# Norms between stages: column halves of the second tile, weights under the root, roots on ScalarE and VectorE

## The reference, cut to what matters

```python
def rms_norm(x, g):                       # and rmsnorm of the second block
    return x * rsqrt(mean(x * x, -1) + EPS) * g

for l in range(DEPTH):                    # first block
    x = x + rms_norm(hybrid_mixer(rms_norm(x, mix_pre), ...), mix_post)
    x = x + rms_norm(memory_cross_attention(rms_norm(x, mem_pre), ...), mem_post)
    x = x + rms_norm(squared_relu_mlp(rms_norm(x, mlp_pre), ...), mlp_post)
h = concat(meta, x)                       # second block, 16 meta tokens ahead
h = h + hybrid_mixer_2(rmsnorm(h, g_mix), ...)
h = h + peer_ffn(rmsnorm(h, g_ffn), ...)
return rmsnorm(h, g_final)[16:]
```

## Time and profile before

| | us |
|---|---|
| median of 3 runs | 1515.65 (1515.44 to 1515.95) |
| the profiled execution, its own time | 1515.26 |
| its span | 1513.5 |
| TensorE busy | 1435.5 (95%) |
| VectorE busy | 1060.0 (70%) |
| ScalarE busy | 757.6 (50%) |
| GpSimd busy | 70.2 (5%) |

### The profile page before, as it was taken

The page is one execution under the profiler, slowest core; times in us unless marked ns, Lnnn a source line. Parts: engine busy times, 40 slices in busy tenths (PEclk is TensorE's granted clock), DMA queues, the critical chain, the costliest instruction groups (busy, mean ns, idle before and its releaser), DMA issues.

```text
span 1513.5 us, 26922 instructions
## 1 busy us (share of the span) xinstructions
PE 1435.5 (95%) x9273; PEld 1293.6 (85%) x9273; DVE 1060.0 (70%) x1981; ACT 757.6 (50%) x1211; POOL 70.2 (5%) x87
## 2 busy tenths in 40 slices
PE   7889889999899997989989999999999999999997
PEld 7867769899798886889979999999999999988886
DVE  6897665555668577569997999555555555567775
ACT  6644654444556533454544555444444444444453
POOL 0200100000000621000000000000000000000000
PEclk9999999999999999999999999999999999999999
DMA  7442325565344522454546888755757566577753
GB/s 280 139 130 96 126 84 188 186 192 183 112 144 161 169 82 70 153 181 154 167 152 185 256 257 259 226 189 184 249 183 245 182 220 210 190 239 249 249 194 140
DMA packets 103208, 274.54 MB, mean 181 GB/s; under 512 B 8160, under 2 KB 41056, under 8 KB 102640
## 3 DMA queue, kind: packets, MB, share of 16 engines
q1 hardware_dynamic: 64832, 237.11, 48.4%
q10 hardware_dynamic: 38032, 34.63, 6.8%
q0 software_dynamic: 288, 2.10, 0.4%
HBM read 254.93 MB, written 18.87 MB: 181 GB/s over the span
## 4 chain that ended last, share of the span: by engine, by line
PE 80%; DVE 15%; ACT 2%; issue 2%; POOL 0%; DMA 0%; POOLq 0%; ACTq 0%; DVEq 0%; SPq 0%
PE Y L1803 43%; PE AO L1803 34%; DVE wl L950 4%; DVE CV L1034 2%; PE M L1803 2%; ACT wh L471 1%; DVE eqs L1558 1%; DVE I L1478 1%; DVE SCO L1494 1%; DVE I L1492 1%; DVE PU L1533 0%; DVE V L1500 0%; DVE V L1486 0%; DVE eqs L1572 0%; DVE xn L973 0%
## 5 line engine op out<-in xcount | busy, mean ns | idle before, releaser
L950 DVE TENSOR_TENSOR wl<-raw,wh 128x1024 fp32r<-128x1024 f32 x440 | 541.6, 1234 | 278.2 <-ACT wh L471 277.4
L471 ACT CAST wh<-raw 128x1024 fp32r<-128x1024 f32 x440 | 460.0, 1048 | 186.7 <-PE AO L1803 92.3
L1803 PE MATMUL AO<-xh,wh 128*128 128x256 f32 (+1 forms) x1776 | 511.0, 288 | 8.6 <-DVE wl L950 7.3
L1803 PE MATMUL AO<-xh,wl 128*128 128x256 f32 (+1 forms) x1776 | 503.4, 283 | 0.0
L1803 PE MATMUL AO<-xl,wh 128*128 128x256 f32 (+1 forms) x1776 | 503.4, 283 | 0.0
L1803 PEld LDWEIGHTS AO<-xh,wh 128*128 128x128 f32 x1776 | 338.5, 191 | 16.3 <-DVE wl L950 9.0
L1803 PEld LDWEIGHTS AO<-xl,wh 128*128 128x128 f32 x1776 | 337.8, 190 | 4.6 <-issue 0.2
L1803 PEld LDWEIGHTS AO<-xh,wl 128*128 128x128 f32 x1776 | 338.7, 191 | 0.0
L1803 PE MATMUL Y<-wh,peer_ah 128*128 128x512 f32 x512 | 200.7, 392 | 2.1 <-DVE peer_al L1620 2.1
L1803 PE MATMUL Y<-wh,peer_al 128*128 128x512 f32 x512 | 200.3, 391 | 0.0
L1803 PE MATMUL Y<-wl,peer_ah 128*128 128x512 f32 x512 | 199.1, 389 | 0.0
(11 more groups left out here) (305 smaller groups left out, 1672.2 us busy)
## 6 DMA issues: line engine op xcount, KB each, us to landing
raw<-in_stream SPq DMA_DIRECT2D x440, 512.0 KB, 3.4
gate_spill<-gstage ACTq DMA_DIRECT2D x32, 512.0 KB, 5.2
gates<-gate_spill ACTq DMA_DIRECT2D x6, 2048.0 KB, 14.9
gates<-gate_spill ACTq DMA_DIRECT2D x8, 512.0 KB, 7.2
rowg<-in_post SPq DMA_DIRECT2D x3, 512.0 KB, 4.4
X<-in_x SPq DMA_DIRECT2D x2, 512.0 KB, 4.8
memx<-in_mem SPq DMA_DIRECT2D x1, 1024.0 KB, 8.1
keys<-in_keys POOLq DMA_DIRECT2D x1, 1024.0 KB, 6.7
```

The costliest lines, as they stand in the source:

```text
L471: nc.scalar.copy(wh[:, s, :], raw[:, s, :]).then_inc(split_hi, 1)
L950: nc.vector.tensor_tensor(wl[:, s, :], raw[:, s, :], wh[:, s, :].bitcast(F32), ALU.subtract)\
L1803: return nc.tensor.matmul(o, a, b, start=start, stop=stop)
```

## The change

- All norms treat tile 1 by two column halves (`HALVES`). `last_two` multiplies tile 1 by halves too: both blocks for columns 0 to 511 (new semaphore `half_rows`), then both for 512 to 1023.
- The post-norm multiplies Y by the weights first (`weighed_rows`), while the squares are summed, and scales by the inverse root together with the residual add (`add_rows`, one multiply-add).
- Squares are taken with scale D^-0.5, so that their sum is the mean. The second half's root gets the first half's sum plus EPS as its bias: GpSimd adds EPS to it (`with_eps`); the accumulated column of the second half is the input.
- The root is a Sqrt on ScalarE, the inverse a reciprocal on VectorE (`inverse`). `root_table` is a tiny Sqrt ahead of each group, which loads the table.
- High and low parts are made for both tiles at once, 256 columns each; TensorE transposes tile 0 into columns 0 to 127 of the eight banks and tile 1 into 128 to 255, with no wait for low parts.
- The meta tile has its own functions and semaphores and keeps GpSimd's inverse root.
- The end works by halves of tile 1 as well, with three output DMAs instead of two.

The diff, cut to its core:

```diff
@@ ScalarE
+            def tile_squares(n, ready):
+                q = NORMS.index(n)
+                ready(0)
+                nc.scalar.activation(junk[:, :], X[:, 0, :], ACT.Square, scale=D ** -0.5,
+                                     accum_out=stat[:, 0:1]).then_inc(tile_ss, 1)
+                act.wait_ge(tile_ss, 3 * q + 1)
+                nc.scalar.activation(stat[:, 8:9], stat[:, 0:1], ACT.Sqrt, bias=eps[:, 0:1]).then_inc(tile_root, 1)
+                for m, h in enumerate(HALVES):
+                    ready(1 + m)
+                    nc.scalar.activation(junk[:, h], X[:, 1, h], ACT.Square, scale=D ** -0.5,
+                                         accum_out=stat[:, 1 + 2 * m:2 + 2 * m]).then_inc(tile_ss, 1)
+                act.wait_ge(tile_ss, 3 * q + 3)
+                act.wait_ge(tile_eps, q + 1)
+                nc.scalar.activation(stat[:, 9:10], stat[:, 3:4], ACT.Sqrt, bias=stat[:, 11:12]).then_inc(tile_root, 1)
+            def tile_high(n):
                 for i in range(KT):
-                    act.wait_ge(tile_turned, KT * (TILE_BASE[n] + TILES[n].index(k)) + (KT if k == 2 else i + 1))
-                    nc.scalar.activation(xh[:, i, c:c + r], turn_bank(n, i, k)[:, 0:r], ACT.Copy,
+                    act.wait_ge(tile_turned, KT * NORMS.index(n) + i + 1)
+                    nc.scalar.activation(xh[:, i, token_cols(n)], turn_bank(n, i)[:, 0:T], ACT.Copy,
+            def root_table():
+                nc.scalar.activation(eps[:, 1:2], eps[:, 0:1], ACT.Sqrt)
...
             def post(p):
+                root_table()
+                act.wait_ge(first_rows, p + 1)
+                square(0, 1, stat[:, 4:5])
+                act.wait_ge(post_y, 4 * p + 1)
+                square(0, 0, eps[:, 2:3])
+                act.wait_ge(post_ss, 4 * p + 2)
+                act.wait_ge(post_eps, 2 * p + 1)
+                nc.scalar.activation(stat[:, 12:13], eps[:, 2:3], ACT.Sqrt, bias=stat[:, 15:16]).then_inc(post_root, 1)
+                act.wait_ge(half_rows, p + 1)
+                square(1, 0, stat[:, 5:6])
+                act.wait_ge(w_used, LAST[STAGE_BEFORE[p + 2]])
+                square(1, 1, stat[:, 6:7])
+                act.wait_ge(post_ss, 4 * p + 4)
+                act.wait_ge(post_eps, 2 * p + 2)
+                nc.scalar.activation(stat[:, 13:14], stat[:, 6:7], ACT.Sqrt, bias=stat[:, 7:8]).then_inc(post_root, 1)
@@ VectorE
             def norm(n):
                 tile_scale(n, 0)
-                tile_low(n, 0, 0, 2)
                 tile_scale(n, 1)
-                tile_low(n, 0, 2, KT)
-                tile_low(n, 1)
+                tile_low(n)
...
             def post(p):
+                dve.wait_ge(first_rows, p + 1)
+                weighed_rows(0, HALVES[0])
+                dve.wait_ge(post_ss, 4 * p + 1)
+                weighed_rows(0, HALVES[1])
+                dve.wait_ge(post_root, 2 * p + 1)
+                inverse(12, post_rstd)
+                dve.wait_ge(post_rstd, 2 * p + 1)
+                dve.wait_ge(post_y, 4 * p + 2)
+                add_rows(0, slice(0, D))
+                dve.wait_ge(post_ss, 4 * p + 3)
+                weighed_rows(1, HALVES[0])
+                dve.wait_ge(post_ss, 4 * p + 4)
+                weighed_rows(1, HALVES[1])
+                dve.wait_ge(post_root, 2 * p + 2)
+                inverse(13, post_rstd)
...
+                for h in HALVES:
+                    add_rows(1, h)
@@ GpSimd
             def norm(n):
-                for k in range(TT):
-                    tile_root(n, k)
+                pool.wait_ge(tile_ss, 3 * NORMS.index(n) + 2)
+                with_eps(11, 1, tile_eps)
@@ TensorE
+            def norm(n):
+                q = NORMS.index(n)
+                for k in range(TT):
+                    for i in range(KT):
+                        if i % (KT // 2) == 0:
+                            pe.wait_ge(tile_scaled, 3 * q + 1 + (0 if k == 0 else 1 + 2 * i // KT))
+                        ins = nc.tensor.transpose(turn_bank(n, i)[:, P * k:P * k + P], xn[:, k, P * i:P * i + P],
+                                                  ident[:, :])
+                        if k:
+                            ins.then_inc(tile_turned, 1)
...
             def last_two(name, ah, al, ready=None):
+                ins.then_inc(first_rows, 1)
+                for half in range(2):
+                    for n, b in enumerate(blocks):
+                        ins = flat(b % SLOTS, [[Y4[1][half]]], [ah(n)[:, P:2 * P]], [al(n)[:, P:2 * P]], (512 * half,),
+                                   False, n == 1)
```

More of the change, by code:

```diff
@@ L509, in norm, with meta_square, meta_high @@
             def norm(n, ready):
[L510 to L514 removed]
+                tile_squares(n, ready)
+                tile_high(n)
+            def meta_square():
+                nc.scalar.activation(xn[0:META, 2, :], metax[:, :], ACT.Square,
+                                     accum_out=stat[0:META, 2:3]).then_inc(meta_ss, 1)
+            def meta_high():
+                act.wait_ge(meta_turned, 1)
+                for i in range(KT):
+                    ins = nc.scalar.activation(xh[:, i, 0:META], meta_bank(i), ACT.Copy,
+                                               scale=gain[:, 4 * KT + i:4 * KT + i + 1])
+                ins.then_inc(meta_hi, 1)
```

261 lines of the change are left out of this document (134 added, 127 removed).

## The result

| | kernel before | changed kernel |
|---|---|---|
| median, us | 1515.55 (1514.17 to 1515.95, 4 runs) | 1498.88 (1497.7 to 1499.31, 4 runs) |
| ratio | | 0.989 [0.9874, 0.9906] |
| profiled execution, its span | 1515.26, 1513.5 | 1499.31, 1497.6 |

Run again, on two chips, the changed kernel had 1498.16 against 1515.22 and 1500.35 against 1515.44: 15 to 17 us.

What follows compares the result with a forecast made beforehand. TensorE, busy for 95% of the span, was taken as the bound, with only its idle places to win; 1.5 + 5.7 + 2.9 + 0.7 = 10.8 us gave a forecast of 1504.8 us, range 1502 to 1508.5 (72%).

Steps and rivals of the forecast that it cites:

- start, to the first matmul: Norm at the start: first matmul moves from 13.27 to about 11.3; taken as 1.5 us (1.2 to 2.1).
- three post-norms, to the first matmul: Each post-norm: first matmul 2.1 us earlier, taken as 1.9 (1.4 to 2.5) after the clock's share; 5.7 in all.
- second mixer, to the first matmul: Norm after the second mixer: first matmul at 659.9 instead of 662.68; 2.9 us (2.1 to 3.9) less the clock's share.
- end: Final norm and output: tile 1's halves end 0.8 us earlier, with one DMA more; taken as 0.7 us (0.3 to 1.3).
- The first transpose: First post-norm: the first transpose comes at 170.0 instead of 171.46, 1.5 us earlier; TensorE's gap becomes 4.5 us.
- From the first transpose to the first matmul: First post-norm: transpose at 170.0, first high part at 172.25, first matmul at about 173.5 instead of 175.57.
- The clock takes a part back: Post-norms: 0.6 us more of the next stage's first block runs at half speed, costing 0.3 us.
- The stages behind keep the head start: Stages after the norms: time won stays won, since TensorE waits for almost nothing after the first blocks; no loss priced.
- Table loads: ScalarE: Sqrt loads ahead of norms are covered and cost nothing; one before the exponentials costs nothing to 1.3 us.
- More gain, by the clock: Rival, at the norms: first block and transposes run at full speed, about 0.8 us more per norm; 1501 us; 8%.
- Square and Sqrt don't share a table: Rival, ScalarE at the norms: each change of function brings a 1.28 us load; slower, 1530 us; 4%.
- No change, given back later: Rival, in later stages: ScalarE's casts or VectorE's bound stages absorb the recovered time; no gain; 3%.

Runs made afterwards that it cites:

- after_fill: The changed kernel with TensorE kept busy in four pauses between stages by products nobody reads (16, 16, 16 and 5); 1500.32 us.
- after_again: The changed kernel unaltered, run again on another chip and day; 1498.16 us.
- before_pool_first: The kernel before with GpSimd's roots of the norm after the second mixer ahead of its two DMA issues; 1515.46 us.
- after_narrow: The changed kernel with high and low parts back at 128 columns per tile and tile 1's transposes again waiting for tile 0's low parts; 1510.97 us.
- after_late: The changed kernel with the first loads of X and of the stream held back by seven GpSimd memsets; 1500.62 us.
- after_old_order: The changed kernel with TensorE's last 24 Y products for tile 1 in the earlier order, block by block, halves inside; 1498.65 us.
- the two of eps: Two runs of the changed kernel with the small buffer eps allocated behind all others instead of among them; 1498.31 and 1500.56 us.
- after_no_preload: The changed kernel without the small square root ahead of each norm that loads the Sqrt table; 1507.21 us.
- before_second: The kernel before unaltered, run again for a second profile; 1515.18 us.
- before_wide_parts: The kernel before with only the 256-column high and low parts and both tiles transposed side by side without waits for low parts; 1509.72 us.
- before_fill: The kernel before with TensorE kept busy in four pauses by products nobody reads (22, 22, 22 and 14); 1514.95 us.
- after_tile1_late: The changed kernel with four VectorE memsets between the scaling of tile 0 and tile 1 in the four norms between stages; 1504.31 us.

## Why the prediction was wrong in size, step by step

Its own steps, for the two profiled executions:

| step | forecast | measured |
|---|---|---|
| start, to the first matmul | 2.0, taken 1.5 | 2.2, of which TensorE loses 0.76 again at 15.22, waiting for VectorE's low part of the next block |
| three post-norms, to the first matmul | 2.1 each, taken 1.9 | 2.9, 3.0, 2.4 (2.5, 2.5, 2.4 between the second profiles) |
| second mixer, to the first matmul | 2.8, taken 2.9 | 3.35 |
| end | 0.7 | 0.45 |
| TensorE's work at 1.2 GHz outside the norms | a loss of some 0.3 each | a gain of 4.1 |
| all else | 0 | a loss of 2.4 (3.6 if the slow work ahead of the clock's records is counted with the clock, a gain of 5.3 then) |
| sum | 10.8 | 15.9 |

So the step that failed is the clock's: a small loss at each norm was forecast and nothing elsewhere, and the clock gave 4.1 us. The second is the price of the norms: 10.1 us forecast, 13.8 measured. The losses in the rest hide a part of both.

- *What bounds the kernel* was right: the gain on the chains came at the five places named and the end. At the end tile 1's output rows are done 3.64 us behind TensorE's last product (1490.27 to 1493.91) instead of 4.67, but the span ends only 0.45 us closer to it; what the third DMA takes of the difference was not traced.
- *The first transpose.* Forecast 4.5 us behind the last Y matmul, measured 4.29, 4.13 and 4.22. VectorE's halves of the residual ended 3.3 us behind it, forecast 3.4.
- *From the first transpose to the first matmul*: the term that was too small. Forecast 3.5 us, measured 2.94, 2.82 and 3.33; in after_fill, at full clock, 2.68. I had the first high part 2.25 us behind the first transpose; it came at 1.80 (168.35, 170.15), and four of the first tile's eight pieces are turned at 2.4 GHz. In after_again, where the slow stretch begins ahead of the first transpose (167.7), the high part comes at 2.19 and the matmul at 3.33, close to the forecast: so what was missed here is the clock again. A part of 256 columns takes 0.47 to 0.50 us on ScalarE, as priced. In before, the first transpose was slow at once (0.66 for a pair), and I had carried that over.
- *The clock takes a part back*: wrong in sign. I reasoned that what is late is late at half speed, so an earlier start only moves work into the slow stretch. The stretch itself got shorter, 3.4 instead of 6.8 us at two post-norms (at all three in the second and third profiles), and gone after the second mixer, where the kernel before has 6.8 (658.0 to 664.8). The first profile also had two stretches fewer behind the small pauses; that part is in some measure luck, as the third profile has as many there as the kernel before (6). I had looked at the clock at the norms alone and not listed it over the whole span, where the kernel before loses 12.8 us of work to it, more than the whole sum I forecast.
- *The stages behind keep the head start*: not wholly. In the first profile TensorE waits 0.76 us at 15.22 (0.87 in the second, not at all in the third) and 0.54 at the MLP's first down product at 218.73 (1.1 and 0.6), where it didn't before; its pauses inside the first mixer add up to some 0.8 us more (2.12 became 2.52, for one; 2.14 in the second profile), and the MLP loses 1.0 by addresses. ScalarE was forecast 0.4 us late at the MLP's first bank; it begins to empty it at 215.39, right behind TensorE's last product for it and without idle time of its own.
- *After the second mixer* the mechanism was as told: GpSimd's small step stands behind the spill's issue (645.80, 646.49), and the second tile is scaled 3.5 us behind the last product, forecast 3.45 to 3.95.
- *The order by halves* was costed at nothing and brings nothing. *Table loads* were costed at nothing and are covered, the one more ahead of the exponentials too (420.76, the next instruction waits 0.51 us for VectorE behind it); the third post-norm needs none. Without their cover they cost 6.0 us between two spans and 8.9 by the medians. The drain of the Trainium skill's page, 3.6 us less gain by the prediction's estimate, didn't show.
- *GpSimd beside VectorE*: forecast 0 to 0.2 us of delay. The step took 0.93 and 0.75 us next to VectorE's instructions, 0.23 where VectorE pauses (646.49); at the norms behind the post-norms ScalarE waited 0.26 us for it before the second root, and TensorE had no wait ahead of the second tile. After the second mixer, where it stands behind the spill, ScalarE waited 0.62 us and TensorE 0.44, as foreseen.
- *The rivals.* "More gain, by the clock" was the one that came, with 8%, and even its 1501 was too high; the range stopped at half of it, at 1502, though the terms at their own high bounds (2.1, 7.5, 3.9 and 1.3) already give 1500.9. The rival was priced at 0.8 us for each norm, for the first block alone, because I took the gain of a norm to be local. "Square and Sqrt don't share a table" falls: of the changed kernel's 32 table loads five belong to the small roots ahead of the norms and the end, and none stands between a Square and a Sqrt. "No change, given back later" is what happened to before_pool_first.

What stays open: what exactly brings a slow stretch. The length of the pause ahead of the first transpose doesn't decide it alone (after_fill has none of the four long pauses and seven stretches elsewhere; after_narrow has the changed kernel's pauses ahead of the first transpose, 14.9 us of slow work, and a granted clock of 0.980 to 0.983 in its eight executions). What goes with it in these profiles is the compact norm as a whole: the seven profiles of kernels with early first transposes, wide parts and no filler or added wait on VectorE, after_late, after_old_order and the two of eps among them, have 8.4 to 12.0 us of slow work (after_no_preload, with later first transposes, 11.4), the seven of before, before_second, before_pool_first, before_wide_parts, before_fill, after_narrow and after_tile1_late 12.8 to 15.8. That is a grouping made afterwards, not a shown cause, and it is weakest for two of them: the profiles of before_wide_parts and before_fill are of slow executions. The other four of before_wide_parts took 4 to 5 us less, at 0.985 instead of 0.982; an estimate from that (0.003 of 1513 us of clock is 4.5 us, off 14.9) puts their slow work near 10 us, among that of the changed kernel.

## What to carry to other kernels

Before pricing a change of TensorE's pauses, list the stretches of low granted clock over the whole span and the work that lies in them: here they gave 4 to 5 us that I had not priced, beside 14 from the chains; a chain made 1.9 us shorter was given back whole, and two halves of a change that bring 4.6 and 5.5 us alone brought 15 to 17 together. Compact the whole restart, from the last product to the first matmul, not one wait in it; filling the four long pauses with idle products didn't move the median. Compare such parts over several profiles, and ask first whether the profiled execution is a typical one. Check a stage's pace after a buffer is added, and load a table under another wait.

## What the runs showed of the hardware that I had not expected

- One kernel's executions differ with the granted clock: before_wide_parts took 1514.54 us at 0.982 and 1509.4 to 1510.4 at 0.985, after_old_order 1503.82 at 0.985 and 1497.58 at 0.991.
- A shift of addresses by at most 32 bytes changed the pace of 1112 matmuls by 1.0 us in 176, and the shift back restored it.
- A GpSimd instruction on one column took 0.93 us beside VectorE's work on SBUF (163.76) and 0.23 without it. The Trainium skill ("GPSIMD Engine Reference", Specifications) says that GpSimd shares its SBUF access with VectorE where that has two SBUF inputs; the trace agrees, VectorE's multiply-add from 163.34 to 164.62 being such an instruction.
